# One decoder block on one core: expert weights fetched as pairs of units, 2 MB with 16 KB runs

## The chip, the core and the metric

The kernel runs on one core of one Trainium2 chip. The metric is the device time of one launch in microseconds, from the median of several runs. The profile is one execution, and its times are given as spans from its first instruction.

## The reference

One block of a decoder for 512 tokens of width 1024: a mixer (gated delta rule heads and causal pooling), then a mixture of 32 experts of which every token picks 4. This document is about the experts. All data are fp32.

```python
def expert_block(args):
    e, tok, wt = args
    xb = xt[tok]
    gu = xb @ w_gate_up[e] + b_gate_up[e]          # w_gate_up[e]: 1024 x 2048
    gate = jnp.minimum(gu[:, :D_EXPERT], SWIGLU_LIMIT)
    up = jnp.clip(gu[:, D_EXPERT:], -SWIGLU_LIMIT, SWIGLU_LIMIT)
    act = (up + 1.0) * gate * jax.nn.sigmoid(SWIGLU_ALPHA * gate)
    yb = act @ w_down[e] + b_down[e]               # w_down[e]: 1024 x 1024
    return yb * wt.astype(yb.dtype)[:, None]
```

The outputs of a token's four experts are added to its row, and a norm ends the block.

## The kernel before

**The mixer** takes about the first 300 us of the span. The change does not touch it.

**Visits.** The tokens of an expert are handled 32 at a time; one such pass over an expert is called a visit here. A table computed on the chip says how many visits each expert has and in which order the experts come, and loops with bounds read from registers (`expert_block`, inside `pe.Fori`) run over them. There are 75 visits in all. Before the first visit of each expert but the first, `expert_bias` forms its bias rows (L1947). A visit on TensorE is then, in this order: `gate_up` (L1972), `gather` of the 32 token rows of the visit after (L1924), `numbers` of its slots (L1933), and `down` with its bias (L2017, L2026). TensorE is split into four column groups of 32, one for each quarter of the output columns, so a product of 128 x 32 weights loaded with 256 columns streamed appears four times for one step.

**Units.** An expert's 12 MB of weights come as `NU` = 12 units of 1 MB, 8 of w_gate_up (`NGU`) and 4 of w_down. A gate-up unit is 128 rows of 8 KB, one to each partition; a down unit is 256 rows of 4 KB, two neighbouring rows to each partition, so 8 KB again. `gate_up` runs over the 8 units for the first half of the columns and, four units behind (`LAG`), for the second half; the products of the second half release the unit in the last visit. The units live in a ring of `RING` = 20 slots. A unit is numbered n = 12 x expert + u, in the order of visiting, and lies in slot n modulo 20.

**The weight stream.** SP issues every unit, in order of n. In `refill` (from L447 on) it waits, for unit n, until unit n - 20 has been used in the last visit of its expert (`w_used`, counted by TensorE), and until the unit four before (`AHEAD`) has landed (L462). So at most four are under way. The issue itself is in `load_unit` (L384). TensorE waits in `landed` (L1939) for a unit's own semaphore before its first product. On this queue there is nothing but the weights during the visits.

**Layouts.** The gathered rows come out of PSUM in the order of the units' rows, so that they can be turned and used as the loaded operand. `quarter` picks the columns of gate and up which one column group computes for one half, and VectorE's `in_order` and `chunked_half` (L1360 to L1367) bring the products into the order in which w_down's rows lie in the partitions. After them VectorE clips, multiplies with the sigmoid of ScalarE and turns the result (L1379); `down` waits for the first half at its first unit and for the second half at its third.

**Results.** GpSimd scatters the rows of a visit with an indirect DMA (L609) on a queue of its own. At the end four 2 MB transfers read these rows back into the ring, 16 KB to each partition, and they are summed and normed.

Of the kernel before, what the change touches and what calls it, by code (L numbers as in the profile page):

```python
# [18 lines left out]
P = 128  # L19
# [12 lines left out]
E, TOPK = 32, 4  # L32
SLOTS = 32
Q = P // SLOTS
QD = D // Q
# [9 lines left out]
UNIT = 2 * D  # L45
NGU = KD
NU = KD + KD // 2
RING = 20
AHEAD = 4
# [4 lines left out]
def moe_block(nc, x, attn_norm_w, w_in, conv_w, a_log, dt_bias, dn_norm_w, pool_w, pool_scale, w_out,  # L54
# [3 lines left out]
    with ctx:  # L58
# [7 lines left out]
        ring = sb("ring", [P, RING * UNIT])  # L66
# [43 lines left out]
        def early(*dims, dt=F32):  # L110
# [28 lines left out]
        h2p = [v.bitcast(BF16).rearrange("p (b d) -> p b d", b=TB) for v in (  # L139
            hbuf[:, 0:TB * D // 2], hbuf[:, TB * D // 2:], aux[:, 0:TB * D // 2])]  # L140
# [85 lines left out]
        ps = ctx.enter_context(nc.psum_tensor("ps", [P, 8, 512], F32))  # L226
# [16 lines left out]

        def quarter(v, q, half):

            pairs = v.rearrange("p s (m r) -> p s m r", r=2 * P)
            return pairs[:, :, 2 * half:2 * half + 2, 2 * SLOTS * q:2 * SLOTS * (q + 1)]

        def in_order(v):

            return v.rearrange("p (m i c) -> p m c i", m=2, c=2)

        def chunked_half(v):

            return v.rearrange("p (m c i) -> p m c i", m=2, c=2)

        def bc(v, n, at):

# [7 lines left out]
        slot_in = [sem(f"slot_in{i}") for i in range(RING)]  # L266
# [27 lines left out]
        gub_used, w_used, gc_ok, uc_step, sg_ok, act_ok, actt_ok, dnb_used, ys_ok, scattered, rowi_ok = [sem(n) for n in (  # L294
            "gub_used", "w_used", "gc_ok", "uc_step", "sg_ok", "act_ok", "actt_ok", "dnb_used", "ys_ok",
            "scattered", "rowi_ok")]
# [15 lines left out]
            link.n = n  # L312
            return link

        def unit_src(e, u):

            if u < NGU:
                return w_gate_up[0, bass.ds(e, 1), u * P:(u + 1) * P, :].rearrange("a p c -> (a p) c")
            r = 2 * P * (u - NGU)
            return w_down[0, bass.ds(e, 1), r:r + 2 * P, :].rearrange("a (p c) n -> (a p) (c n)", c=2)  # L320

        def unit_dst(slot, u):
            return ring[:, slot * UNIT:(slot + 1) * UNIT]

        def slot_of(j, u):

            return (NU * j + u) % RING, (NU * j + u) // RING
# [34 lines left out]
        def _(sp):  # L362
# [17 lines left out]
            sp.dma_start(poolw[:, :, :], pool_w[0].rearrange("g c d -> c g d")).then_inc(pool_router_in, 16)  # L380
            sp.dma_start(wrt[:, :, :], w_router[0].rearrange("(k p) e -> p k e", p=P)).then_inc(pool_router_in, 16)

            def load_unit(e, u, slot):
                sp.dma_start(unit_dst(slot, u), unit_src(e, u)).then_inc(slot_in[slot], 16)  # L384

            load_unit(0, 0, 0)
            sp.wait_ge(proj_ps, 2)
# [59 lines left out]
            def refill(e):  # L447


                used = sp.value_load(tab[0:1, e + USED:e + USED + 1], min_val=0, max_val=MAXB * NU)  # L450
                following = {ne: sp.value_load(tab[0:1, VISIT + e + ne:VISIT + e + ne + 1], min_val=0, max_val=E - 1)
                             for ne in (1, 2) if e + ne < E}
                for u in range(NU):
                    n = NU * e + u + RING
                    if n >= NU * E:
                        continue

                    landed = n - AHEAD
                    sp.wait_ge(w_used, used + (u + 1))
                    if e == 0 and u >= NGU:  # L460
                        sp.wait_ge(side_ps, 2 + u + 1 - NGU)
                    sp.wait_ge(slot_in[landed % RING], (landed // RING + 1) * 16)  # L462
                    load_unit(following[n // NU - e], n % NU, n % RING)

            for e in range(E - 1):
                refill(e)
# [1017 lines left out]
        def _(pe):  # L1484
            mm, tr = nc.tensor.matmul, nc.tensor.transpose
# [5 lines left out]
            for b in range(TB):  # L1491
                pe.wait_ge(x_in[b], 16)
                for k in range(KD - 1):
                    last = x_transposed(b, k, k)
# [7 lines left out]
            for b in range(TB):  # L1502
                pe.wait_ge(xdiag_ok, b + 1)
                last = mm(bank(7)[:, b * P:(b + 1) * P], ones, xdiag[:, b, :], start=True, stop=True)
# [263 lines left out]
            for n in range(NCH):  # L1768
                for hh in range(2):
                    last = mm(ps[rows(hh), 7, 4 * n:4 * n + 4], ba_part[:, CH * n:CH * (n + 1)], S4[:, hh:2 * H:2],  # L1770
                              start=True, stop=True)
# [4 lines left out]
            for i, c in enumerate((causal, same, first, second)):  # L1776
                last = mm(ps[:, 7, 64 + i * NC:64 + (i + 1) * NC], c, gt[:, 8], start=True, stop=True)
# [3 lines left out]
            for a in range(2):  # L1781
                last = mm(bank(2 + a, 8), same, GUM[:, group(a)], start=True, stop=True)
# [10 lines left out]
            for a in range(2):  # L1793
                last = mm(bank(2 + a, 8), later, BI[:, group(a)], start=True, stop=True)
# [21 lines left out]
            for n in range(NCH):  # L1816
                for hp in range(2):
                    for hh in range(2):
                        c = 2 * n + hp
# [35 lines left out]
            for n in range(1, 6):  # L1855
                m, lo = (NQKV + H + 1) + (n - 1) // 2, 4 * ((n - 1) % 2)
# [26 lines left out]
            for b in range(TB - 1):  # L1883
                n = 2 * b + 2
# [28 lines left out]
            def gather(count, free, hot=hot, blocks=TB, pieces=None):  # L1913

                pe.wait_ge(hot_ok, count)
                if free is not None:
                    pe.wait_ge(xgt_ok, free)
                if pieces is not None:
                    pe.wait_ge(h2p_ok, pieces)
                for b in range(blocks):  # L1920
                    for n in range(3):
                        for q in range(Q):
                            rows = h2p[n][:, b, :].rearrange("p (j r) -> p j r", r=P)[:, :, SLOTS * q:SLOTS * (q + 1)]
                            last = mm(ps[SLOTS * q:SLOTS * (q + 1), 2, 0:QD].rearrange("p (j i) -> p j i", i=SLOTS),  # L1924
                                      hot[:, b, 0, :], rows, start=b == 0 and n == 0, stop=b == blocks - 1 and n == 2)
                last.then_inc(gat_ps, 1)

# [7 lines left out]
                last.then_inc(idx_ps, 1)  # L1935

            def landed(e, u):
                slot, turn = slot_of(e, u)
                pe.wait_ge(slot_in[slot], (turn + 1) * 16)  # L1939
                return ring[:, slot * UNIT:(slot + 1) * UNIT].rearrange("p (s c) -> p s c", s=2)  # L1940

            def bias_rows_of(to, start, stop):

                bias = bias3[:, 0:2 * D].rearrange("p (s c) -> p s c", s=2)
                for half in range(2):
                    for q in range(Q):
                        last = mm(to(half)[SLOTS * q:SLOTS * (q + 1)].rearrange("p (s m r) -> p s m r", s=2, m=2),  # L1947
                                  selu[:, :], quarter(bias, q, half), start=start, stop=stop)
                return last

# [17 lines left out]
            def gate_up_unit(e, u, half, banks, x, skip, opens, opened):  # L1968

                w = landed(e, u)  # L1970
                for q in range(Q):
                    last = mm(ps[SLOTS * q:SLOTS * (q + 1), banks[half], 0:2 * P].rearrange(  # L1972
                        "p (s m r) -> p s m r", s=2, m=2), x[:, SLOTS * u:SLOTS * (u + 1)],
                        quarter(w, q, half), start=opens and u == 0, stop=u == NGU - 1)
                if opened is not None and u == 0 and half == 0:
                    last.then_inc(opened, 1)
                if half:
                    last.then_inc(w_used, 1 + (skip if u == NGU - 1 else 0))
                elif u == NGU - 1:
                    last.then_inc(gu_half, 1)  # L1980
# [139 lines left out]
```

## Time and profile before

| | us |
|---|---|
| median of 3 runs | 1310.0 |
| lowest and highest | 1307.76, 1312.25 |
| the profiled execution | 1305.44 |
| its span, first to last instruction | 1303.6 |
| TensorE busy | 1251.8 |
| VectorE busy | 556.9 |
| ScalarE busy | 238.7 |
| bytes read from HBM | 432.53 MB |

The span is what the views below show; the 1.8 us around it belong to the run. TensorE's busy time comes from pipelined products whose ends are modelled. The rows further down give start times in microseconds of the span.

### The profile page before, as it was taken

To read this page: it belongs to the slowest core of one execution; us is meant where nothing else is said; L and a number is where in the kernel's file an instruction comes from. 1 tells how busy PE (TensorE), PEld (TensorE's weight loads), DVE (VectorE), ACT (ScalarE), POOL (GpSimd) and SP (SyncE) were. 2 spreads that over 40 slices of the span, in tenths; PEclk is the share of its full clock that TensorE was granted. 3 is DMA by queue.
4 is the path that set the end of the run, shared out by engine and by line. 5 is a ranking of instruction groups with operands and counts; after the bars stand their busy time and mean duration, and the time that the engine had idled before them with its cause. 6 is when DMAs were issued, how large, how long until landed. Compare 5 with 4: busy or idle time off the path is not lost.

```text
span 1303.6 us, 53095 instructions
## 1 busy us (share of the span) xinstructions
PE 1251.8 (96%) x21477; PEld 770.5 (59%) x21477; DVE 556.9 (43%) x2029; ACT 238.7 (18%) x587; POOL 162.2 (12%) x267
## 2 busy tenths in 40 slices
PE   8999999999999999999999999999999999988885
PEld 4546655545666666666665666666666665645552
DVE  5454223447344344444343443443443443433337
ACT  3431123332111111111111111111111111111112
POOL 4100430122101101101101001011011011000110
PEclk9999999999999999999999999999999999999998
DMA  7453131619999999999999999999999999999997
GB/s 236 139 191 130 34 130 49 258 65 355 394 419 409 421 419 421 420 420 416 421 420 420 412 422 417 421 415 419 421 411 423 416 420 414 421 420 421 420 424 282
DMA packets 80505, 455.75 MB, mean 350 GB/s; under 512 B 11057, under 2 KB 23018, under 8 KB 30730
## 3 DMA queue, kind: packets, MB, share of 16 engines
q1 hardware_dynamic: 76400, 445.69, 83.9%
q0 software_dynamic: 3888, 8.40, 1.8%
q8 instruction: 87, 1.43, 0.4%
q14 instruction: 24, 0.20, 0.0%
q10 hardware_dynamic: 106, 0.04, 0.0%
HBM read 432.53 MB, written 23.27 MB: 350 GB/s over the span
## 4 chain that ended last, share of the span: by engine, by line
DMA 48%; PE 46%; DVE 2%; issue 1%; SPq 0%; POOL 0%; DVEq 0%; ACT 0%; POOLq 0%; ACTq 0%
DMA ring<-in_w_gate_up_dram 30%; DMA ring<-in_w_down_dram 15%; PE ps L1972 14%; PE ps L1526 11%; PE ps L2026 7%; PE ps L1546 4%; PE ps L1924 3%; PE ps L1587 2%; DMA x_rows_dram<-cat,rowi 1%; PE ps L1580 1%; DMA pair_rows_dram<-cat,rowi 1%; DMA ring<-x_rows_dram 0%; DMA pair_rows_dram<-cat,sm 0%; PE ps L1488 0%; PE ps L2017 0%
## 5 line engine op out<-in xcount | busy, mean ns | idle before, releaser
L1972 PE MATMUL ps<-ring,cat 128*32 128x256 f32 x9856 | 551.1, 380 | 8.9 <-DMA ring<-in_w_gate_up_dram 8.7
L1972 PEld LDWEIGHTS ps<-ring,cat 128*32 128x32 f32 x9856 | 334.2, 110 | 204.1 <-DMA ring<-in_w_gate_up_dram 12.1
L2026 PE MATMUL ps<-ring,cat 128*32 128x256 f32 x4800 | 277.6, 380 | 18.5 <-DMA ring<-in_w_down_dram 15.9
L2026 PEld LDWEIGHTS ps<-ring,cat 128*32 128x32 f32 x4800 | 142.2, 110 | 125.2 <-DMA ring<-in_w_down_dram 16.0
L1526 PE MATMUL ps<-hbuf,ring 128*128 128x512 f32 x320 | 146.0, 601 | 1.7 <-DVE hbuf L944 1.7
L1335 DVE TENSOR_REDUCE wslot<-ps 128x2 f32<-128x6 f32 x75 | 12.3, 164 | 292.5 <-ACT cat L869 291.0
L842 ACT ACTIVATE cat<-cat 128x128 f32<-128x128 f32 x154 | 47.7, 310 | 481.9 <-DVE cat L1370 461.0
L609 POOL DMA_INDIRECT pair_rows_dram<-cat,rowi x73 | 72.7, 996 | 435.4 <-ACT cat L869 435.4
L1924 PE MATMUL ps<-hbuf,cat 128*32 128x256 bf16 x2432 | 105.7, 273 | 0.6 <-DVE cat L1444 0.6
L1526 PEld LDWEIGHTS ps<-hbuf,ring 128*128 128x128 f32 x320 | 58.2, 190 | 67.2 <-issue 65.5
L869 ACT ACTIVATE cat<-ps,wslot 128x256 f32<-128x256 f32 x75 | 35.5, 473 | 336.5 <-PE ps L2026 331.6
L1365 DVE TENSOR_TENSOR cat<-ps,cat 128x128 f32<-128x128 f32 x148 | 43.1, 291 | 115.2 <-PE ps L1972 111.6
L1924 PE MATMUL ps<-aux,cat 128*32 128x256 bf16 x1216 | 91.0, 273 | 0.0
L1924 PEld LDWEIGHTS ps<-hbuf,cat 128*32 128x32 bf16 x2432 | 71.7, 97 | 14.3 <-DVE cat L1444 1.1
L1439 DVE COPY selu<-E 96x32 bf16 x75 | 13.3, 178 | 125.1 <-issue 125.1
L605 POOL TENSOR_TENSOR rowi<-rowj,qcol 128x1 int32<-128x1 int32 x75 | 15.4, 206 | 409.8 <-DMA pair_rows_dram<-cat,rowi 393.1
L1546 PE MATMUL ps<-ring,cat 128*128 128x512 f32 x128 | 58.6, 599 | 0.9 <-issue 0.9
L855 ACT ACTIVATE cat<-ps 128x256 f32<-128x256 f32 x148 | 55.5, 375 | 15.8 <-PE ps L1972 10.3
L1444 DVE TENSOR_TENSOR cat<-iotaf,rank 128x512 bf16 x75 | 51.9, 692 | 12.0 <-DVE gie L1440 12.0
L1379 DVE STREAM_TRANSPOSE cat<-cat 128x128 f32<-128x128 f32 x154 | 48.0, 312 | 5.3
L1375 DVE SCALAR_TENSOR_TENSOR cat<-cat 128x128 f32<-128x128 f32 x154 | 45.7, 297 | 5.3
L1378 DVE TENSOR_TENSOR cat<-cat 128x128 f32<-128x128 f32 x154 | 45.3, 294 | 5.2
(376 smaller groups left out, 903.3 us busy)
## 6 DMA issues: line engine op xcount, KB each, us to landing
ring<-in_w_gate_up_dram SPq DMA_DIRECT2D x256, 1024.0 KB, 10.0
ring<-in_w_down_dram SPq DMA_DIRECT2D x128, 1024.0 KB, 9.8
ring<-in_w_in_dram SPq DMA_DIRECT2D x10, 1024.0 KB, 6.4
pair_rows_dram<-cat SPq DMA_DIRECT2D x4, 2048.0 KB, 11.0
ring<-pair_rows_dram SPq DMA_DIRECT2D x4, 2048.0 KB, 20.6
ring<-in_w_out_dram SPq DMA_DIRECT2D x1, 4096.0 KB, 13.0
ring<-in_x_dram SPq DMA_DIRECT2D x4, 512.0 KB, 5.0
x_rows_dram<-ring SPq DMA_DIRECT2D x2, 1024.0 KB, 10.0
```

Of the source, the lines that this page charges most:

```text
L609: G.indirect_dma_start(out=into, out_offset=bass.IndirectOffsetOnAxis(ap=rowi[:, 0:1], axis=0), in_=ys, in_offset=None, bounds_check=limit ...
L842: A(sg[:, half], gc[:, half], ACT.Sigmoid, scale=ALPHA).then_inc(sg_ok, 1)
L855: A(biased[half], ps[:, BIAS, 2 * P * half:2 * P * (half + 1)], ACT.Copy).then_inc(bias_copied, 1)
L1375: step(V.scalar_tensor_tensor(out=uc[:, half], in0=uc[:, half], scalar=1.0, in1=gc[:, half], op0=ALU.add, op1=ALU.mult), uc_step, n * 4 + 4)
L1378: step(V.tensor_tensor(act_[:, half], uc[:, half], sg[:, half], ALU.mult), act_ok, n + 1)
L1379: V.transpose(to[:, half], act_[:, half]).then_inc(told, by)
L1444: step(V.tensor_tensor(hot[:, :, :, :], slots, mine, ALU.is_equal), hot_ok, count)
L1526: last = mm(bank(m % 2), win[:, piece % 3, k, m % 2 * P:(m % 2 + 1) * P], hT[:, k, :], start=k == 0, stop=k == KD - 1)
L1546: last = mm(bank(n % 2), catT[:, k, b * P:(b + 1) * P], wout[:, k, 512 * half:512 * (half + 1)], start=i == 0, stop=i == KD - 1)
L1924: last = mm(ps[SLOTS * q:SLOTS * (q + 1), 2, 0:QD].rearrange("p (j i) -> p j i", i=SLOTS), hot[:, b, 0, :], rows, start=b == 0 and n == 0, ...
L1972: last = mm(ps[SLOTS * q:SLOTS * (q + 1), banks[half], 0:2 * P].rearrange("p (s m r) -> p s m r", s=2, m=2), x[:, SLOTS * u:SLOTS * (u + 1 ...
L2026: last = mm(ps[SLOTS * q:SLOTS * (q + 1), 1, 0:QD], actT[:, c // 4, SLOTS * (c % 4):SLOTS * (c % 4 + 1)], w[:, i, q * QD:(q + 1) * QD], st ...
```

## The change

Two neighbouring units become one transfer of 2 MB where the first has an even number n of at least 32 and below 372: that is from the slots that follow the first twenty units and the second expert's own, to the end of the last expert but one. The units before and after keep their single transfers.

- Each partition holds 16 KB that lie together in memory, two rows of w_gate_up or four rows of w_down, split over two neighbouring slots. The single units take the same layout, so a single unit now fetches one 8 KB half of each 16 KB run.
- SP waits for both slots of a pair to be used, and for the landing of what unit n - 4 came with. `arrival` says which semaphore carries a unit's landing and up to which count. TensorE waits for the pair's landing before either unit.
- The gathered rows are read with a step of two bf16 elements (4 bytes), since a gate-up unit now holds every other row. Their places in PSUM stay contiguous.
- w_down's partitions now hold four neighbouring rows. So `quarter` picks one run of 128 columns instead of two of 64, for the bias rows as well, and VectorE's `in_order` reads its 128 columns with a step of four fp32 instead of two.

```diff
         def quarter(v, q, half):
-            pairs = v.rearrange("p s (m r) -> p s m r", r=2 * P)
-            return pairs[:, :, 2 * half:2 * half + 2, 2 * SLOTS * q:2 * SLOTS * (q + 1)]
+            fours = v.rearrange("p s (m r) -> p s m r", r=4 * P)
+            return fours[:, :, half, P * q:P * (q + 1)]
         def in_order(v):
-            return v.rearrange("p (m i c) -> p m c i", m=2, c=2)
+            return v.rearrange("p (i c) -> p c i", c=4)
         def chunked_half(v):
-            return v.rearrange("p (m c i) -> p m c i", m=2, c=2)
+            return v.rearrange("p (c i) -> p c i", c=4)
...
-        def unit_src(e, u):
+        def unit_src(e, u, units=1):
             if u < NGU:
-                return w_gate_up[0, bass.ds(e, 1), u * P:(u + 1) * P, :].rearrange("a p c -> (a p) c")
-            r = 2 * P * (u - NGU)
-            return w_down[0, bass.ds(e, 1), r:r + 2 * P, :].rearrange("a (p c) n -> (a p) (c n)", c=2)
-
-        def unit_dst(slot, u):
-            return ring[:, slot * UNIT:(slot + 1) * UNIT]
+                r = 2 * P * (u // 2)
+                rows = w_gate_up[0, bass.ds(e, 1), r:r + 2 * P, :].rearrange("a (p c) n -> (a p) (c n)", c=2)
+            else:
+                r = 4 * P * ((u - NGU) // 2)
+                rows = w_down[0, bass.ds(e, 1), r:r + 4 * P, :].rearrange("a (p c) n -> (a p) (c n)", c=4)
+            return rows[:, u % 2 * UNIT:(u % 2 + units) * UNIT]
+
+        def unit_dst(slot, units=1):
+            return ring[:, slot * UNIT:(slot + units) * UNIT]
+
+        def doubled(n):
+            return RING + NU <= n < NU * (E - 1) and n % 2 == 0
+
+        def arrival(n):
+            lead = n - 1 if n % 2 and doubled(n - 1) else n
+            loads = [k for k in range(lead % RING, lead + 1, RING) if not (k % 2 and doubled(k - 1))]
+            return slot_in[lead % RING], 16 * len(loads)
...
-            def load_unit(e, u, slot):
-                sp.dma_start(unit_dst(slot, u), unit_src(e, u)).then_inc(slot_in[slot], 16)
+            def load_unit(e, u, slot, units=1):
+                sp.dma_start(unit_dst(slot, units), unit_src(e, u, units)).then_inc(slot_in[slot], 16)
...
                     n = NU * e + u + RING
-                    if n >= NU * E:
+                    if n >= NU * E or n % 2 and doubled(n - 1):
                         continue
-                    landed = n - AHEAD
-                    sp.wait_ge(w_used, used + (u + 1))
+                    units = 2 if doubled(n) else 1
+                    signal, count = arrival(n - AHEAD)
+                    sp.wait_ge(w_used, used + (u + units))
                     if e == 0 and u >= NGU:
                         sp.wait_ge(side_ps, 2 + u + 1 - NGU)
-                    sp.wait_ge(slot_in[landed % RING], (landed // RING + 1) * 16)
-                    load_unit(following[n // NU - e], n % NU, n % RING)
+                    sp.wait_ge(signal, count)
+                    load_unit(following[n // NU - e], n % NU, n % RING, units)
...
-                            rows = h2p[n][:, b, :].rearrange("p (j r) -> p j r", r=P)[:, :, SLOTS * q:SLOTS * (q + 1)]
-                            last = mm(ps[SLOTS * q:SLOTS * (q + 1), 2, 0:QD].rearrange("p (j i) -> p j i", i=SLOTS),
+                            rows = h2p[n][:, b, :].rearrange("p (m r c) -> p m c r", r=P, c=2)[:, :, :, SLOTS * q:SLOTS * (q + 1)]
+                            last = mm(ps[SLOTS * q:SLOTS * (q + 1), 2, 0:QD].rearrange("p (m c i) -> p m c i", c=2, i=SLOTS),
                                       hot[:, b, 0, :], rows, start=b == 0 and n == 0, stop=b == blocks - 1 and n == 2)
...
-                slot, turn = slot_of(e, u)
-                pe.wait_ge(slot_in[slot], (turn + 1) * 16)
+                slot, _ = slot_of(e, u)
+                pe.wait_ge(*arrival(NU * e + u))
```

## Rows read from the trace of the kernel before

**Rows 1.** The page: TensorE's busy time, and DMA share in 40 slices.

```profile
PE 1251.8 (96%) x21477; PEld 770.5 (59%) x21477; DVE 556.9 (43%) x2029; ACT 238.7 (18%) x587; POOL 162.2 (12%) x267
...
DMA  7453131619999999999999999999999999999997
```

**Rows 2.** Busy time by stretch: stretch, its length, engines' busy time, clock, DMA share, GB/s.

```profile
389.00:1105.00 716.00, 711.45 (x14612) 454.02 (x14608) 300.40 (x1276) 101.40 (x290) 69.81 (x116) 1.00 1.01 418
1105.00:1266.00 161.00, 140.76 (x2804) 88.29 (x2800) 56.98 (x242) 19.70 (x56) 13.36 (x24) 0.99 1.01 421
```

**Rows 3.** The chain, 700 to 800 us: start, duration, what; one visit, 60.96 later another.

```profile
735.39 0.22 PE ps L1947 x8
735.62 6.94 PE ps L1972 x128
742.55 1.31 PE ps L1924 x48
743.86 0.19 PE ps L1933 x4
...
744.27 3.46 PE ps L2026 x64
...
796.35 0.22 PE ps L1947 x8
```

**Rows 4.** Timeline of TensorE at two experts' starts: start, length, engine, line, operation.

```profile
488.88 0.39 PE L1947 MATMUL ps<-cat,selu 96*32 96x256 bf16 x8
...
1105.40 0.39 PE L1947 MATMUL ps<-cat,selu 96*32 96x256 bf16 x8
```

**Rows 5.** TensorE's waits, 389 to 1105 us: total us, times, longest.

```profile
PE ps L2026 <- DMA ring<-in_w_down_dram: 4.4, 5, 1.4
```

**Rows 6.** DMA queues, 500 to 620 us: packets, MB, share of 16 engines.

```profile
q1 hardware_dynamic: 6739, 49.06, 98.3%
q0 software_dynamic: 480, 1.07, 2.3%
q8 instruction: 8, 0.13, 0.4%
```

**Rows 7.** The same for 1266 to 1270 and 1266 to 1271 us.

```profile
q1 hardware_dynamic: 119, 1.70, 100.8%
...
q1 hardware_dynamic: 144, 2.10, 99.1%
```

**Rows 8.** Line L384, all unit transfers: from issue to landing.

```profile
DMA to landing us min/median/max: 4.7/10.0/11.4
```

**Rows 9.** The chain, 610 to 800 us, three of its transfers.

```profile
658.53 10.03 DMA ring<-in_w_gate_up_dram
...
668.77 9.72 DMA ring<-in_w_down_dram
...
698.87 11.24 DMA ring<-in_w_down_dram
```

**Rows 10.** Timeline of SP: four unit issues, the first at 663.65 us.

```profile
663.65 5.45 SPq L384 DMA_DIRECT2D ring<-in_w_down_dram  x4
```

**Rows 11.** Timeline of SP, 330 to 372 us: the issues before and from unit 32.

```profile
329.83 18.67 SPq L384 DMA_DIRECT2D ring<-in_w_gate_up_dram  x8
356.71 2.76 SPq L384 DMA_DIRECT2D ring<-in_w_down_dram  x4
```

**Rows 12.** Groups by line and form: total busy us, mean ns, idle before.

```profile
L1526 PE MATMUL ps<-hbuf,ring 128*128 128x512 f32 x320 | 146.0, 601 | 1.7 <-DVE hbuf L944 1.7
...
L1365 DVE TENSOR_TENSOR cat<-ps,cat 128x128 f32<-128x128 f32 x148 | 43.1, 291 | 115.2 <-PE ps L1972 111.6 <-ACT cat L855 3.6
```

**Rows 13.** Timeline of VectorE in the visit of rows 3: the second half's transpose.

```profile
744.05 0.31 DVE L1379 STREAM_TRANSPOSE cat<-cat 128x128 f32<-128x128 f32 x1
```

**Rows 14.** The chain from 1105 us: the last weight unit.

```profile
1254.59 9.73 DMA ring<-in_w_down_dram
```

More of the change, by code:

```diff
@@ L1946, in bias_rows_of @@
                     for q in range(Q):
-                        last = mm(to(half)[SLOTS * q:SLOTS * (q + 1)].rearrange("p (s m r) -> p s m r", s=2, m=2),
+                        last = mm(to(half)[SLOTS * q:SLOTS * (q + 1)].rearrange("p (s r) -> p s r", s=2),
                                   selu[:, :], quarter(bias, q, half), start=start, stop=stop)
@@ L1972, in gate_up_unit @@
                     last = mm(ps[SLOTS * q:SLOTS * (q + 1), banks[half], 0:2 * P].rearrange(
-                        "p (s m r) -> p s m r", s=2, m=2), x[:, SLOTS * u:SLOTS * (u + 1)],
+                        "p (s r) -> p s r", s=2), x[:, SLOTS * u:SLOTS * (u + 1)],
                         quarter(w, q, half), start=opens and u == 0, stop=u == NGU - 1)
```

## The prediction

> **What bounds the kernel now.** I read the summary rows of the page first. TensorE is busy 96% of the span and the 16 DMA engines stand at 9 tenths in every slice from the twelfth on [rows 1]. A page with two full resources does not say which one sets the end, so I went on to stretches. From 389 to 1105 us TensorE is busy 711.5 of 716 us and the DMA share is 1.01, at 418 GB/s; from 1105 to 1266 us TensorE is busy only 140.8 of 161 us and the DMA share is still 1.01, at 421 GB/s [rows 2]. In the second stretch the weight stream alone is the limit. In the first the two are nearly level, and their two cycle times have to be compared.
>
> The experts there alternate between three and two visits. By the chain, a visit is 6.94 (gate and up) + 1.31 (gather) + 0.41 (slot numbers and down bias, 743.86 to 744.27) + 3.46 (down) = 12.1 us, and an expert adds 0.22 for its bias [rows 3]. Five visits without a wait run from 735.39 to 796.35: 60.96 us [rows 3]. Ten such cycles really take from 488.88 to 1105.40, where the bias products of two experts 20 apart start: 61.65 us each [rows 4]. So TensorE loses 0.69 us a cycle, 6.9 us in ten. The waits view names 4.4 us of it, all on w_down landings [rows 5]; the rest is too short to be listed.
>
> The stream needs, per cycle of 24 units: q1 moves 49.06 MB in 98.3% of 16 engines x 120 us [rows 6], that is 38.47 us of one engine per MB, or 2.52 us per 1 MB unit (1.0486 MB over 16 engines), 60.5 us for 24. Scatters and instruction fetches take another 2.3 + 0.4% [rows 6], 1.7 us of a cycle. The shares add up to 101.0%, so this sum overcounts by 1%: 62.2 / 1.01 = 61.6, which is the 61.65 measured. **The DMA engines set the pace all along, and TensorE stands 0.7 us per cycle behind them.** A faster stream pays in full after 1105 us, and at most 0.7 us per cycle before it.
>
> **The change part by part.** *Longer packets.* Units 32 to 371 go as 170 pairs. The trace has transfers of just this form, the four 2048 KB reads of the pair rows into the ring, in a stretch where next to nothing else runs: 1.70 MB in 100.8% of 16 x 4 us, and 2.10 MB in 99.1% of 16 x 5 us, so 37.9 and 37.8 us of an engine per MB; 119 packets for 1.70 MB, completion marks included, are 14.3 KB each, against 7.3 KB in the weight stretch [rows 6, 7]. A unit would cost 2.49 to 2.47 us against 2.52: 0.035 to 0.047 us less, 0.07 to 0.09 per pair, half of the completion marks included. I take 0.07, since the windows are short and rounded. 170 x 0.07 = 12 us is the ceiling; 26 pairs lie behind the last ring-full pause (units 320 to 371), where it counts in full: 26 x 0.07 = **1.8 us**. In the middle 12 pairs save 0.84 per cycle. The stream falls from 61.65 to 60.8, just under TensorE's 60.96. A tie is not met exactly, since pauses of one meet pauses of the other; I take 61.15, a gain of 0.5 per cycle. 389 to 1105 us holds 11.5 cycles: **5.7 us**.
>
> The Trainium skill (DMA: Bandwidth & Descriptors, Anatomy of one DMA) fits a transfer by a fixed 2.0 us plus its bytes at 436 GB/s. If every transfer paid that in turn, 170 fewer would save 340 us. The trace bears the fixed part out only for a lone transfer and not for a queue.
>
> In the rows: the shortest unit takes 4.7 us from issue to landing, the median one 10.0 [rows 8], and the chain steps from one w_gate_up landing to the one four units later in 668.77 - 658.53 = 10.2 us [rows 9]. What 4.7 has beyond 2.5 of data, 2.2 us, is the latency, and it hides behind three units that are already queued.
>
> *Waiting for two slots, and for the landing four units back.* SP now waits until both slots are used: one unit's products later, 6.94 / 8 = 0.87 us. Behind this wait on SP are only further units. It matters when the ring is full: the last visit of a three-visit expert has to free the first slot. At 658.5 us SP issues a unit, the next comes at 663.65 [rows 10], and the former lands only at 658.53 + 10.03 = 668.56 [rows 9]; 4.9 us of work were still queued. With 0.87 less it is 4.0, against 2.2 of latency: the engines stay fed, cost 0. If TensorE becomes the slower side this cover shrinks to nothing, and the engines idle, but then they have time to spare. In the other place, at unit 32, the last issue before ends at 348.50 us and the next begins at 356.71 [rows 11]; by the median landing the queue is empty at 358.5, so cover is 1.8, already under the latency, and 0.87 later gives **+0.9 us** (0 to 0.9). The check four units back now leaves one pair, 5 us, queued at each issue, instead of three units, 7.5 us: more than 2.2, cost 0; a slow packet on one engine is evened out less. Bound: the chain has one late landing, 11.24 against 10.0 [rows 9], and it is where TensorE waited; if one in each of 6 pairs of cycles were lost in full, 1.2 x 6 = 7 us.
>
> *A unit is there only when its pair is.* TensorE now waits at unit 10 of an expert for what it needed at unit 11, 3.46 / 4 = 0.87 us earlier. The slack around this loop: from the release of unit 0 in the last visit (six of 16 half units, 2.6 us in) to the need of unit 11 in the next three-visit expert TensorE has 9.5 (rest of the visit) + 24.4 (two visits and a bias) + 11.4 (a visit and bias less one down unit) = 45.3 us; the stream has 16 units to land, 2.2 + 16 x 2.52 = 42.5 from an empty queue. Slack 2.8 before; 2.8 - 0.87 - 0.87 + 0.6 (16 x 0.035) = 1.7 after. It takes up a late landing of 1.2 us but not two. This shifts TensorE once and does not repeat. Units 372 to 383 stay single, so the end sees nothing of it: 0 to +0.9, I take 0.
>
> *The gather.* The 48 bf16 products of a visit now read columns with a step of two elements. No operation before does this with bf16. They take 1.31 / 48 = 27 ns each; the fp32 products, whose elements lie 4 bytes apart as these will, take 6.94 / 128 = 54 ns [rows 3]. Bounds: 0 to +27 ns, 0 to 1.28 us per visit. Below nothing is excluded, since the number of columns stays. I take 0: a 512-column fp32 product of L1526 that fills the array costs 146.0 / 320 = 456 ns, 0.89 ns a column, with one stream read, while four fp32 quarters read four streams in 4 x 54 = 216 ns for 256 columns, 0.84 ns a column [rows 3, 12]. Four times the reading costs nothing, so fp32's factor of two looks like arithmetic and not like reading.
>
> The Trainium skill (SBUF — State Buffer, Door 1: The DMA port swizzle) says that SBUF reads want at least two hits per 16-byte line. Four bf16 elements at the new step share such a line, so by it the gather costs 0 too; no row before shows this.
>
> *VectorE.* in_order steps by four fp32 instead of two, in four operations of a visit (L1365 and L1367 for each half; L1365 takes 291 ns [rows 12]). The Trainium skill's page just named leaves it open: two hits per line are gone at a step of 16 bytes, yet it lists a step of four fp32 as free.
>
> Bounds by the rows: 0, or a doubled duration, at most 0.29 each, 0.58 per half. The second half's transpose starts at 744.05 and lasts 0.31 [rows 13]; the product that needs it, unit 10, starts half of down's 3.46 after 744.27, at 746.0 [rows 3]. Cover 1.6 us; cost 0 either way. The gate-up and bias products read longer runs, which are no fewer columns: 0.
>
> **Sum** against the profiled execution, 1305.4 us (span 1303.6): -5.7 - 1.8 + 0.9 = -6.6, rounded to -7, so 1298. It lies 4.6 below the median of the three runs, 1310.0, which themselves span 4.5 us. On the median: **1303 us**.
>
> **Rivals.** *A, the lead lost eats the gain (same).* Each ring-full pause idles the engines for the 0.87 of the pair's release: 11.5 x 0.87 = 10 against 12 saved, or the late landings cost their 7 us. Net 0 to -3: about 1308. For it: TensorE is as near as 0.7 us per cycle, so a faster stream soon runs into the full ring. Against: 4.9 us were queued at the pause. *B, the packets are not cheaper (same).* The 37.8 us per MB comes from 5 us of trace, with no scatter beside it; then about 1309. That the transfer is cut into 8 KB packets anyway, so that the change does not do what it says, is nearly excluded by [rows 7]. *C, the strided gather (slower).* At its full price a cycle is 60.96 + 5 x 1.28 = 67.4 of TensorE, 5.7 over now, 11.5 cycles: +66, some 1375. It decides early: from (61.65 - 60.96) / 5 = 0.14 us a visit, 3 ns a product, TensorE alone is as slow as the kernel now. After 1105 us it is free, since two visits then take 26.8 of about 30 us per expert. *D, coarser queueing (slower).* With pairs the slowest engine's delay is passed on to all; the middle gains nothing and loses 7 us to late landings, and both one-time shifts of 0.9 come on top, less 1.8 of the tail: +7, 1317.
>
> **How the numbers follow.** Forecast 0.55 (1298 to 1306 on the median), A 0.17, B 0.11, C 0.08, D 0.09. A measurement of this kernel tells about 0.3%, 4 us. Faster by more: the forecast's 0.55 less its weak end, 0.04, plus 0.04 of A: 0.55. Within: 0.29. Slower: C and nearly all of D: 0.16. The range takes in the ceiling of the stream, 12 us and a bit for the runs' spread (1297), A and B, and D up to 1316; C's full price is left out.
>
> **What would show it.** The issues table should have 170 fewer ring transfers, and 2048 KB ones with a median landing still near 10 us. q1 should fall below 38 us of an engine per MB; if it stays at 38.5, B. L1924's products should stay at 1.31 us per 48; 2.6 is C. Ten cycles should take 61.0 to 61.3 us each. A DMA share clearly under 1.00 in 389 to 1105 us with TensorE waits gone is TensorE as the limit, as forecast; the share down with waits still there is A or D. The last weight unit should land about 7 us sooner than 1254.59 + 9.73 = 1264.3 [rows 14]. A price of bytes that does not carry over to weights, or a cycle over 61.6, would make the forecast wrong.

## The result and the profile after

The changed kernel takes **1328.6 us** (1327.6 to 1332.1) against 1310.1 (1307.8 to 1312.3): a ratio of 1.0146, 95% interval 1.0121 to 1.0172. I had forecast 1303, faster. It is 18.5 us slower, and outside the range.

The stretch from 389 to 1105 us in the changed kernel, to be read against [rows 2]; the columns are the stretch, its length, the engines' busy times, the clock, the DMA share and GB/s:

```profile
389.00:1105.00 716.00, 701.52 (x14192) 451.94 (x14187) 314.30 (x1240) 98.45 (x281) 66.62 (x113) 0.99 0.99 407
```

The stream became slower: 407 GB/s against 418, and the engines' share fell from 1.01 to 0.99. TensorE did 701.5 us of work there against 711.5, and it waited more for the weights; its waits in the same stretch, against [rows 5]:

```profile
PE ps L2040 <- DMA ring<-in_w_down_dram: 14.3, 10, 2.6
```

The starts of the experts of [rows 4], on TensorE's timeline:

```profile
494.27 0.39 PE L1961 MATMUL ps<-cat,selu 96*32 96x256 bf16 x8
...
1129.47 0.39 PE L1961 MATMUL ps<-cat,selu 96*32 96x256 bf16 x8
```

Ten cycles take 635.2 us, 63.5 each against 61.65. Of the 22.2 us by which the span grew (1325.8 against 1303.6), 5.4 are there by 494, 18.7 come in these ten cycles, and the rest gives 1.9 back, 0.9 of it up to the last unit, which lands at 1287.4 (1264.3 before, [rows 14]):

```profile
1277.46 9.99 DMA ring<-in_w_down_dram
```

The loss is uneven: in this trace six of the ten cycles take 61.6 to 62.6 us and four take 65.3 to 65.7; before, all ten took 61.0 to 62.6. Of the 5.4 us by 494, 1.6 are there at the first bias products of the span (302.6 against 301.0), before any pair. About 2.8 come at unit 32. SP issues the first pair 3.8 us later than unit 32 came in [rows 11]:

```profile
360.47 2.06 SPq L397 DMA_DIRECT2D ring<-in_w_down_dram  x2
```

Between 350 and 370 us the engines idle for 4.6 us, against 1.8 before (counted as in the table below).

The queue rows for 389 to 1105 us, changed kernel first, then before:

```profile
q1 hardware_dynamic: 19553, 284.78, 96.4%
```

```profile
q1 hardware_dynamic: 40115, 292.17, 98.2%
```

Packets are half as many, and the page lists 170 transfers of 2048 KB, so the change does what it says. Yet an engine spends 0.964 x 16 x 716 / 284.78 = 38.8 us per MB, against 38.5 before; I had forecast 37.8. The groups of L1924, L1365 and L1360, now L1938, L1379 and L1374 (total busy, mean ns):

```profile
L1938 PE MATMUL ps<-hbuf,cat 128*32 128x256 bf16 x2432 | 111.5, 275 | 0.0
...
L1379 DVE TENSOR_TENSOR cat<-ps,cat 128x128 f32<-128x128 f32 x148 | 57.2, 387 | 98.5 <-PE ps L1986 87.8 <-PE ps L2040 3.7
...
L1374 DVE TENSOR_SCALAR cat<-ps 128x128 f32<-128x128 f32 x6 | 1.7, 276 | 0.1
```

The gather keeps its pace (275 ns against 273). VectorE pays 96 ns for the step of four fp32 at L1379, within the bound of 290, and hidden. L1379 reads two operands with this step, the products in PSUM and the bias rows in SBUF. L1374 reads the products alone, with the same step, and takes 276 ns against 277 before. So the step is free where PSUM alone is read, and costs where an operand in SBUF is read with it; the two operations differ (TENSOR_SCALAR, TENSOR_TENSOR), so the split is not a clean one.

### The profile page after: what moved, and what is told of

It reads as the page before. It is cut to its first block, busy times and chain, and to the rows that moved or that the text cites. A ratio compares the mean times of both kernels' runs of the same rounds, so it can differ in the third digit from the quotient of the medians.

```text
span 1325.8 us, 52244 instructions
## 1 busy us (share of the span) xinstructions
PE 1268.7 (96%) x21476; PEld 785.9 (59%) x21477; DVE 585.3 (44%) x2029; ACT 239.0 (18%) x587; POOL 162.7 (12%) x267
## 4 chain that ended last, share of the span: by engine, by line
DMA 50%; PE 46%; DVE 2%; issue 1%; SPq 0%; POOL 0%; ACT 0%; POOLq 0%; DVEq 0%; ACTq 0%
DMA ring<-in_w_gate_up_dram 29%; DMA ring<-in_w_down_dram 19%; PE ps L1986 14%; PE ps L1540 11%; PE ps L2040 7%; PE ps L1560 4%; PE ps L1938 2%; PE ps L1601 2%; DMA x_rows_dram<-cat,rowi 1%; PE ps L1594 1%; PE ps L2020 1%; PE ps L1502 0%; DMA ring<-x_rows_dram 0%; DVE ring L1493 0%; PE ps L1686 0%
## 5 line engine op out<-in xcount | busy, mean ns | idle before, releaser
L1986 PE MATMUL ps<-ring,cat 128*32 128x256 f32 x9856 | 555.5, 382 | 4.5 <-DMA ring<-in_w_gate_up_dram 4.3
L1986 PEld LDWEIGHTS ps<-ring,cat 128*32 128x32 f32 x9856 | 342.2, 111 | 197.8 <-issue 10.2
L2040 PE MATMUL ps<-ring,cat 128*32 128x256 f32 x4800 | 283.9, 386 | 29.7 <-DMA ring<-in_w_down_dram 27.3
L2040 PEld LDWEIGHTS ps<-ring,cat 128*32 128x32 f32 x4800 | 145.6, 111 | 137.0 <-issue 38.6
L1938 PE MATMUL ps<-hbuf,cat 128*32 128x256 bf16 x2432 | 111.5, 275 | 0.0
L1379 DVE TENSOR_TENSOR cat<-ps,cat 128x128 f32<-128x128 f32 x148 | 57.2, 387 | 98.5 <-PE ps L1986 87.8
L1938 PE MATMUL ps<-aux,cat 128*32 128x256 bf16 x1216 | 96.3, 275 | 0.0
L1938 PEld LDWEIGHTS ps<-hbuf,cat 128*32 128x32 bf16 x2432 | 75.7, 95 | 13.9 <-DVE cat L1458 0.4
L869 ACT ACTIVATE cat<-ps 128x256 f32<-128x256 f32 x148 | 55.6, 376 | 17.8 <-PE ps L1986 12.5
L1381 DVE TENSOR_TENSOR cat<-ps,cat 128x128 f32<-128x128 f32 x148 | 56.5, 382 | 0.0
```

The source lines that it names most:

```text
L869: A(biased[half], ps[:, BIAS, 2 * P * half:2 * P * (half + 1)], ACT.Copy).then_inc(bias_copied, 1)
L1379: V.tensor_tensor(chunked_half(gc[:, half]), in_order(ps[:, b, 0:P]), in_order(bias[half][:, 0:P]), ALU.add).then_inc(uc_step, 1)
L1381: V.tensor_tensor(chunked_half(uc[:, half]), in_order(ps[:, b, P:2 * P]), in_order(bias[half][:, P:2 * P]), ALU.add).then_inc(uc_step, 1)
L2040: last = mm(ps[SLOTS * q:SLOTS * (q + 1), 1, 0:QD], actT[:, c // 4, SLOTS * (c % 4):SLOTS * (c % 4 + 1)], w[:, i, q * QD:(q + 1) * QD], st ...
```

## The packet records

To see where the engines' time goes I took the single packets of the weight queue between 389 and 1105 us (the trace has them; no view lists them). Idle is the time in which fewer than 16 packets run, over 16. Slow is what packets take beyond 50 ns over their usual 309 (8 KB) or 611 ns (16 KB), counted in full and over 16. A pause is where SP waits for the full ring, from 3 us before the issue to 5 us after it.

| us of all 16 engines | idle at pauses | idle elsewhere | slow at pauses | slow elsewhere |
|---|---|---|---|---|
| before | 2.4 | 0.0 | 2.9 | 1.9 |
| changed | 9.0 | 3.0 | 7.0 | 17.3 |

The sum is 36.3 against 7.2, 29.1 us more. Packets that are not slow take 611.9 ns (16 KB) and 312.2 ns (8 KB) on average in these two traces, so the long ones save (2 x 312.2 - 611.9) ns x 17381 / 16 = 13.5 us. Net 15.6. For the 292.17 MB of the kernel before, the changed one would need 716 x (292.17 / 284.78 - 1) = 18.6 us longer; the account explains all but 3 us of it. So the packets are cheaper, as forecast, when they run undisturbed; 6% of them do not (0.7% before), and most of these take up to twice as long. Two suspects fall out of the table: the pauses, and something between them.

By the landing marks on the units' semaphores, the first and the last of the 16 engines end a transfer 2.6 us apart before and 2.1 us in the changed kernel (medians), and in the stretch I followed SP has issued the next pair about 1.0 us after the last engine's end. The slow packets between the pauses have their time: of their 17.3 us, 11.6 lie in packets that start 1.5 to 3.0 us after SP's last issue. With pairs six ahead, a run below, it is 0.4 of 1.8 us.

## Experiments

### Which part of the change

**The stream alone.** SP issues 84 units per stage with the same landing check; nothing else runs.

> The weight stream alone, nothing else on the core: six stages of 84 MB from the expert weights into the 20-slot ring, each ended before the next begins. In order: 1 MB with 8 KB runs (as before), 2 MB with 16 KB runs (as changed), 2 MB with two 8 KB runs per partition, 1 MB with 8 KB halves of 16 KB runs, 2 MB with 16 KB runs and six units ahead in place of four, and the first form again. The rest of the computation is left out. Theory 1 (16 KB packets are themselves delayed in memory): stages 1, 3, 4 and 6 take about 84 x 2.49 = 209 us at 420 GB/s, stages 2 and 5 take 2 to 3% longer, 213 to 216 us, whatever the depth. Theory 2 (a landing that gates 2 MB starves engines): stages 2 and 3 are both slow, 213 to 216 us, and stage 5 comes back to 206 to 209. Theory 3 (the loss needs the other engines or the scatters beside it): all stages within 1%, the 16 KB ones at 206 us as predicted from the pair rows.

Inside the first two stages (stretch, length, GpSimd, clock, DMA share, GB/s); stages 3, 4 and 6 read 422 GB/s as the first, and stage 5 reads 429 as the second:

```profile
10.00:200.00 190.00, 0.00 (x0) 1.00 1.01 422
220.00:410.00 190.00, 0.00 (x0) 1.00 1.01 429
```

The queue rows of the first two:

```profile
q1 hardware_dynamic: 11009, 80.18, 101.3%
```

```profile
q1 hardware_dynamic: 5582, 81.48, 100.7%
```

That is 38.4 and 37.6 us of an engine per MB. 16 KB packets gain 429 / 422 = 1.7%, all that was forecast and more. Pairs four ahead lose nothing by themselves. Theory 3 holds as far as this: the loss needs the rest of the kernel.

**Pairs without long packets**, in the kernel before (w_down's source likewise, and the waits of the change with them):

```diff
-                return w_gate_up[0, bass.ds(e, 1), u * P:(u + 1) * P, :].rearrange("a p c -> (a p) c")
+                return w_gate_up[0, bass.ds(e, 1), u * P:(u + units) * P, :].rearrange("a (k p) c -> (a p) k c", k=units)
```

> The kernel before with its own layouts, but the same 170 pairs of 2 MB, the same waits for two slots and for a pair's landing; each partition gets two separate 8 KB runs. Theory 1 (16 KB packets): as before, 1310 +- 4 us. Theory 2 (coarse waits and queueing): all or most of the loss, 1324 to 1329 us, with a DMA share clearly under 1.01 in 389 to 1105 us.

1336.1 us, ratio 1.020 (1.016 to 1.024): theory 2, and more than it asked for. The stretch:

```profile
389.00:1105.00 716.00, 693.55 (x14171) 448.30 (x14164) 292.70 (x1243) 98.79 (x283) 67.17 (x112) 1.00 1.00 404
```

TensorE's granted clock is 1.00 in this stretch and 0.99 in the changed kernel, so the clock is not what makes pairs slow.

**Layouts without pairs:**

```diff
-            return RING + NU <= n < NU * (E - 1) and n % 2 == 0
+            return False
```

> The changed kernel with no unit doubled: its layouts, its gather with a step of two, VectorE's step of four, and single 1 MB transfers that fetch 8 KB halves of 16 KB runs. Theories 1 and 2: 1310 +- 4 us, since neither long packets nor pairs are left; VectorE's four operations stay at about 385 ns and cost nothing. Rival (the layout or the addresses cost): 1320 us or more.

1309.9 us, ratio 1.000 (0.998 to 1.002). Layouts, gather, the 8 KB halves and the slower VectorE cost nothing. With the run above, the whole loss and more is in the pairs, and the long packets take 7.5 us of it back (1336.1 to 1328.6, medians). In the two profiled executions the ten cycles take 63.5 us each with either, so these 7.5 us are not seen in that stretch.

**Three pairs under way:**

```diff
-AHEAD = 4
+AHEAD = 6
```

> The changed kernel with the landing check six units back in place of four, so three pairs under way. Theory 2 (engines starve while the slowest ends a pair): the DMA share in 389 to 1105 us returns from 0.99 to 1.01 and the time falls to 1308 to 1315 us. Theory 1 (the packets themselves): it stays above 1322 us.

1312.3 us, ratio 1.002 (1.001 to 1.004): 16 of the 18.5 us are back. Of what was expected the share did not come, it stays at 0.99:

```profile
389.00:1105.00 716.00, 712.51 (x14518) 459.59 (x14516) 321.97 (x1270) 101.02 (x289) 68.19 (x116) 1.00 0.99 416
```

The packet table says why: slow elsewhere is down to 1.8 us and idle elsewhere to 0.0, but the pauses keep 10.4 of idle and 8.5 of slow. One pause, as the 40 slices of 660 to 680 us, half a microsecond each:

```profile
DMA  9999999999799997774195499999999999999999
```

The engines run dry to a tenth. They are ahead of TensorE here, and the ring is full. This is the forecast's TensorE limit, but only with six ahead, and only nearly: the ten cycles take 61.95 us each, not 61.15, and TensorE still waits 3.0 us for w_down in the stretch.

### Is it the time left in the queue?

**Single units, three ahead.** `AHEAD = 3` in the kernel before.

> The kernel before with single 1 MB transfers, but each issued when the unit three back has landed, so that two units, 5 us, are queued at an issue, as much as one pair leaves. Theory 2a (what counts is the work left queued on every engine when the next is issued): as slow as the pairs, 1322 to 1336 us. Theory 2b (the landing of 2 MB and the wait for two slots count, not the depth): 1310 +- 4 us.

1313.2 us, ratio 1.005 (1.003 to 1.008): theory 2b by the number, yet slower beyond the measurement. With as much queued as one pair leaves, single units lose 5 us and not 18. The loss is unsteady: ten executions range from 1307.7 to 1326.1 us, those of the kernel before beside them from 1305.7 to 1312.6.

**Single units, two ahead.** `AHEAD = 2`.

> The kernel before with the landing check two units back: one unit, 2.5 us, is left in the queue at an issue. With a latency of 2.2 us and the first and last engine 2 us apart (the traces' landings) most engines run dry at each issue: 1400 us or more, against 1313 with 5 us left and 1309 with 7.5. Rival (the depth hardly matters): under 1330 us.

1423.8 us, ratio 1.086 (1.082 to 1.090). So the cost is a cliff: 7.5 us queued at an issue costs nothing, 5 us costs 5, 2.5 us costs 115.

**Single units, six ahead**, the control.

> The kernel before with the landing check six units back: the control for the depth alone. With 7.5 us queued at an issue no engine runs dry between pauses, so 1309 +- 3 us. If it is faster by 4 us or more, what the pairs six ahead recover is the depth's own gain.

1309.8 us, ratio 1.001 (0.999 to 1.002). Depth has no gain of its own. (The check six back leaves five units queued, 12.5 us; 7.5 is what four back leaves.)

**The stream alone, each issue held back.** GpSimd waits for the landing, runs memsets of 0.95 us and then lets SP issue.

> The weight stream alone, each issue after the first few held back behind the landing that allows it by one or two 0.95 us memsets on GpSimd (about 1.4 and 2.4 us with the signals); the rest is left out. Six stages of 84 MB: pairs of 16 KB runs four ahead, held by 0, 1 and 2 memsets; 1 MB units three ahead, held by 1 and 2; pairs six ahead held by 2. Theory Q (a queue that has under about 2 us left at an issue makes slow first packets): stage 1 takes 207 us, stage 2 209 to 213, stage 3 over 220, stage 6 207; mean packet above 630 ns in stages 2 and 3. If pairs bear it worse than single units, stages 4 and 5 lose clearly less than 2 and 3 against 210; if it is the time alone, they lose the same share. Rival (not the queue): all stages within 1% of 207 and 210.

```profile
10.00:200.00 190.00, 0.00 (x0) 1.00 1.01 429
220.00:430.00 210.00, 40.26 (x77) 1.00 0.99 386
450.00:675.00 225.00, 77.48 (x117) 1.00 0.95 365
695.00:910.00 215.00, 81.74 (x156) 1.00 0.98 380
930.00:1170.00 240.00, 155.87 (x234) 1.00 0.93 342
1190.00:1380.00 190.00, 76.01 (x114) 1.00 1.01 429
```

This is the clearest reading. From first to last packet the stages took 207, 230, 243, 234, 258 and 208 us: theory Q, with more lost in the second stage than its 209 to 213. By the trace SP issues 1.2 us after the landing with one memset and 2.2 us with two, at once without. Pairs four ahead fall from 429 to 386 GB/s with one, and to 365 with two. The queue row of the second stage:

```profile
q1 hardware_dynamic: 5564, 80.94, 98.6%
```

That is 0.986 x 16 x 210 / 80.94 = 40.9 us of an engine per MB, at a share of 0.99: most of the loss hides in slow packets and the engines look busy. It is the changed kernel's picture, stronger (38.8, 0.99). Six ahead, the same delay of two memsets costs nothing, so the memsets themselves do not slow the stream. Single units three ahead fall as far, to 380 and 342, so pairs as such are not worse (their 422 undelayed was taken four ahead; three ahead has no undelayed stage). What counts is how much is still queued when the next issue comes. That it is each engine's own share that counts fits the time at which the slow packets come, but a packet record does not name its engine. The delay also drives the engines apart: they end a transfer 0.6 us apart in the first stage and 2.5 us in the second.

### What shortens that time in the kernel?

**The scatters.** GpSimd's DMA of every visit becomes a memset of `rowi`, in the changed kernel and in the one before. The loss is the difference of the two.

> The changed kernel with the visits' indirect DMAs on GpSimd's queue left out (their rows are not stored, so the result lacks the experts after the first visits). Theory 2a with the scatters as what puts the 16 engines out of step: the loss against the kernel before is gone, TensorE becomes the limit in 389 to 1105 us (61.2 us per cycle), total 1290 to 1300. Rival (the engines fall out of step through something else, instruction fetches or the pauses of a full ring): scattered slow packets stay and it takes 1312 us or more.

> The control for the one above: the kernel before without the same indirect DMAs. The stream saves their 2.3% and TensorE becomes the limit: cycles of 61.0 us, total 1296 to 1302 us. Under theory 2a with the scatters as cause both controls agree within 4 us, under the rival the changed one is 12 us or more slower.

1306.2 and 1291.8 us (ratios 0.998 and 0.987, within 0.995 to 1.000 and 0.984 to 0.989). The loss is 14.4 us in place of 18.5, which is the rival's 12 or more, though 1306.2 lies between the two ranges given for it and 1291.8 is 4 us below its own. The scatters are at most a small part. Before without them reaches TensorE's own pace, so its stream could be faster still, and the 14.4 us rather understate what pairs cost the stream:

```profile
389.00:1105.00 716.00, 715.83 (x14724) 454.28 (x14720) 302.43 (x1285) 102.43 (x292) 16.88 (x118) 1.00 1.00 412
```

**Stores beside the stream alone:**

> The six stages of the stream kernel again, with a 128 KB store from SBUF on GpSimd's queue beside it about every 10 us; everything else is left out. Theory 2a with the scatters as cause: the two stages of pairs four units ahead lose 2% or more against the single units (stage 2: 213 us or more, in place of 207 + 4 for the stores' own bytes), and the stage six ahead does not. Rival: stages 2 and 5 stay equal, at 209 to 211 us.

```profile
10.00:200.00 190.00, 104.66 (x124) 1.00 1.01 423
232.00:432.00 200.00, 98.27 (x117) 1.00 1.01 429
```

The bytes of the stores are in these rates. The stage of pairs took 217 us, more than the 213 of the theory, but the single units slowed as well, to 221, and the pairs keep their 1.6%; pairs of two 8 KB runs took 220. So stores are not what costs the pairs; the rival's equal stages did not come either, since the stores ended before the fifth.

**Long packets on two engines, beside the stream alone:**

> The weight stream alone with a load of two 16 KB packets on GpSimd's queue every 11 to 13 us beside it (the traces of the full kernels show an instruction fetch of 16 KB, 1.0 us long, about every 15 us); the rest is left out. Six stages of 84 MB: 1 MB units four ahead, 2 MB pairs of 16 KB runs four ahead, 1 MB units three ahead, 2 MB pairs of 8 KB runs four ahead, both kinds of pairs six ahead. Theory F (packets that delay one engine at a time put the engines out of step, and pairs four ahead cannot even it out): stages 2 and 4 take 213 us or more, against 207 and 210 in the stream alone, stage 3 stays within 2 us of stage 1, stages 5 and 6 are back at 208 and 211. Rival (something else in the kernel): stage 2 stays under 210 us and stage 4 under 212.

> The same with the load repeated about every 4 to 5 us, three times the dose. Theory F: the loss of the pairs four ahead grows with the dose, stages 2 and 4 at 218 us or more, and stays under 3 us of that six ahead. Rival: all six stages gain the same 1 to 2 us for the bytes that were added.

All six stages of the dense run had the load. Inside the stages the rates were 358, 361, 352, 354, 366 and 361 GB/s; the second and the fifth, pairs four and six ahead:

```profile
270.00:500.00 230.00, 48.80 (x66) 1.00 0.96 361
...
1035.00:1270.00 235.00, 51.76 (x70) 1.00 0.96 366
```

All forms lose about 15%, single units as well, and pairs six ahead are hardly better than pairs four ahead (366 and 361). In the sparser run four ahead gave 237 us for either kind of pairs and 239 for single units, and the load had ended by the last two stages, which can't be used. So theory F falls in this form. I think that the two loaded engines were the same every time, and were then simply the slowest; the runs do not show it.

### The pauses, and a better version

**Units 8 and 9 of each expert single**, so that a pause ends at the release of one unit:

```diff
-            return RING + NU <= n < NU * (E - 1) and n % 2 == 0
+            return RING + NU <= n < NU * (E - 1) and n % 2 == 0 and n % NU != NGU
```

> The changed kernel, but units 8 and 9 of every expert come singly: they are the ones that wait for the first slots that come free after a full ring. So a pause ends at the release of one unit, as before. Theory P (0.87 us lost at each of about 12 pauses by the wait for two slots, from the traces 16 us of idle and slow first packets there against 5 before): 1318 to 1321 us. Rival (pauses do not matter, the whole loss is the coarse queue): 1326 to 1329 us.

1325.9 us, ratio 1.012 (1.010 to 1.015): the rival's range, only 2.7 below the changed kernel. Four ahead the pauses matter little in the end, though the table has them at 11 us: a good part of what is not lost there is lost between them. Idle and slow time at the pauses falls from 16.0 to 9.7 us, and elsewhere it rises from 20.3 to 23.2.

**The same, six ahead:**

> The same with the landing check six units back. Theory P and theory 2 together leave only the cheaper 16 KB packets: 1303 to 1307 us, below the kernel before. If TensorE is the limit in the middle anyway and its visits are 0.04 us longer with the new gather, it stays at 1308 to 1312 us.

**1306.4 us**, ratio 0.9975 (0.9957 to 0.9994): below both kernels, if by little. It is 6 us below the pairs six ahead without the single units (5.3 when each is held against the kernel before of its own round), so the wait for two slots does cost there. Its stretch, in which TensorE has next to no time left to win:

```profile
389.00:1105.00 716.00, 714.47 (x14647) 460.48 (x14640) 325.69 (x1287) 102.31 (x293) 68.65 (x117) 1.00 1.00 418
```

**Pairs of 8 KB runs, six ahead:**

> Pairs with two 8 KB runs per partition, the layouts of before, six units ahead. If depth alone cures the coarse queue: 1312 to 1318 us, from 1336 four ahead; the pauses still lose their 0.87 us each. If the packets' length matters as well, it stays 4 us or more above the 1312 of the 16 KB pairs six ahead.

1318.9 us, ratio 1.007 (1.005 to 1.010), 17 below the same pairs four ahead. Depth cures either kind, and the long packets are worth another 6.6 us.

## Why the prediction was wrong

The step that failed is **the check four units back**. It was priced at 0: the check "now leaves one pair, 5 us, queued at each issue, instead of three units, 7.5 us: more than 2.2, cost 0". Two things were wrong in it. The 5 us are what the slowest engine has left; the first one ended its share 2.1 us earlier, and the issue came 1.0 us after the last one's end. That leaves it 4.9 - 2.1 - 1.0 = 1.8 us, an estimate from medians, against 7.5 - 2.6 - 1.0 = 3.9 before. And the price of coming below the 2.2 us was not mainly idle engines but slow packets, which I had no row for: 24.3 us of them against 4.8, idle 12.0 against 2.4. The held-back stream shows how steep it is, 429 to 386 GB/s for 1.2 us less. The kernel, from 418 to 407 GB/s, sits at the edge of this cliff, and six ahead gave 16 of the 18.5 us back. Why a late issue makes packets slow is not shown. Rival D named the mechanism with 0.09 and had the time, +7 instead of +18.5, too low: it counted only the late landings of [rows 9] and two shifts of 0.9.

*The wait for two slots*, priced at 0 from a cover of 4.0 us, was the second miss, by the same error: of the unit that lands at 668.56 the first engine had marked its share at 664.94, 1.3 us after the issue at 663.65 from which I counted 4.9 us of cover. At unit 32 the term was +0.9, and the engines idle 2.8 us longer there. At the pauses idle and slow grew by 10.7 us, 0.9 for each of 12, the 0.87 us of rival A. But four ahead its removal gave 2.7 us, and only six ahead the 6 us. So A's mechanism is real and its price depends on D's.

*A unit only when its pair is there*, priced at 0: no run tests it alone. The pairs six ahead with units 8 and 9 single still have it for all other units and lose nothing.

*Longer packets* were right: 611.9 against 624.4 ns for two, 429 against 422 GB/s alone, 6.6 to 7.5 us in the kernel between like versions. The ceiling of 12 us was not reached. Six ahead TensorE as the limit can explain that; four ahead it stays open. Rival B is refuted, though its sign, 38.5 us of an engine per MB, came true with 38.8: that number holds the slow packets too.

*The pace of the two cycles*, 61.65 and 60.96 us, was right and useful: the kernel before without the scatters ran at TensorE's pace, 715.8 of 716 us busy. The expected share under 1.00 with waits gone came, nearly, only six ahead (0.99, waits of 3.0 us); at 0.99 with 14.3 us of waits it was the sign named for A or D.

*The gather, VectorE, the layouts*: 0 as forecast, shown by layouts without pairs. Rival C is refuted (275 ns). That agrees with the Trainium skill (SBUF — State Buffer, Door 1: The DMA port swizzle) on its two hits per line. Of the two readings that this page allows for a step of four fp32, the trace agrees with the one that costs something: 387 against 291 ns with an operand in SBUF, 276 against 277 with none.

*The tail*: 0.9 us gained up to the last unit, of the 1.8 forecast.

**What stays open.** Single units three ahead have about the same left in the queue as pairs four ahead, and in the held-back stream they fare no better; in the kernel they lose 5 us against 18 or 26. By the same estimate their first engine has 5.0 - 2.0 - 1.0 = 2.0 us left, hardly more than 1.8; whether so little on so steep a cliff makes the difference is not shown. And what drives the engines 2.1 to 2.6 us apart in the kernels, 0.5 to 1.6 in the stages of the stream alone, is not found: late issues do it in the held-back stream, but the kernel before has no late ones; not the scatters, not stores beside the stream; single packets on changing engines, such as instruction fetches, were not tried cleanly.

## What to carry to other kernels

When transfers are made larger, count the look-ahead in bytes still queued on the *first* engine to finish when the next issue comes, not in transfers: with the same limit of 4 MB under way, doubling the size cut what is left at the issue from 7.5 to 5 us, and on the first engine, by the estimate above, from 3.9 to 1.8. Raise the limit along with the size (here six units, which cost nothing). Where the larger transfer also waits for a release, keep the transfer that ends a pause small. A slow-packet price shows as a growing time per MB at a DMA share near 1; a look at the share alone misses it.

## What the hardware showed that I had not expected

- A starved queue shows first as slow packets and hardly as idle engines: 98.6% share at 40.9 us per MB, against 100.7% at 37.6 for the undisturbed pairs.
- The cliff is steep: 1309, 1313 and 1424 us for single units four, three and two ahead.
- With nothing else running a 16 KB packet takes 615 ns and an 8 KB one 313 (medians), which gives 429 against 422 GB/s with all 16 engines on weights.
- A VectorE operation on 128 columns that reads PSUM and SBUF with a step of four fp32 takes 387 ns, with a step of two 291. Reading PSUM alone it takes 276 and 277.
